# A two-block network on one core: retention values turned to token rows by a transpose, each head's mean taken off while the banks are read

## The reference

```python
proj = u @ w_in
rq, rk, rv, rg, a_cq, a_ckv, a_kr, a_gret, a_gmla = jnp.split(proj, SPLIT_IDX, axis=-1)
rv = rv.reshape(B, L, RET_HEADS, RET_DV)
y_ret = _head_group_norm(_bidir_retention(rq, rk, rv, decay_f, decay_b), gn_w)
y_ret = (jax.nn.silu(rg) * y_ret) @ w_ret_out

def _head_group_norm(y, w):
    mu = jnp.mean(yf, axis=-1, keepdims=True)
    var = jnp.mean(jnp.square(yf - mu), axis=-1, keepdims=True)
    yn = ((yf - mu) * lax.rsqrt(var + GN_EPS)).reshape(B, L, H * dv)
```

## Time and profile before

| | us |
|---|---|
| median of 3 runs | 1061.37 |
| lowest and highest of them | 1061.02, 1061.76 |
| the profiled execution, its own time | 1061.51 |
| its span, first to last instruction | 1059.7 |

### The profile page before, as it was taken

One profiled execution on the slowest core, in us unless ns is written; L12 is line 12 of the kernel. 1 busy time (PEld: TensorE's weight loads), 2 busy tenths in 40 slices (PEclk: granted clock), 3 DMA queues, 4 the chain that ended last, 5 costly groups with the idle time before them and its releaser, 6 DMA issues.

```text
span 1059.7 us, 19331 instructions
## 1 busy us (share of the span) xinstructions
PE 1041.0 (98%) x7716; PEld 963.7 (91%) x7716; DVE 745.9 (70%) x810; ACT 548.0 (52%) x589; POOL 2.2 (0%) x5
## 2 busy tenths in 40 slices
PE   8999999999999999999999999999999999999998
PEld 7998997899999999989889999999898997888887
DVE  6855747768766666678767766666788987766673
ACT  6422536545644444465796444444576574444442
POOL 0000000000000000000000000000000000000000
PEclk8999999999999999999999999999999999999999
DMA  9894242345556666666416455465353444646531
GB/s 304 234 205 147 80 140 80 120 140 166 170 173 180 191 195 196 186 201 224 134 41 238 159 195 201 158 207 190 120 160 120 163 156 158 236 160 204 192 119 40
DMA packets 162589, 177.11 MB, mean 167 GB/s; under 512 B 4800, under 2 KB 148288, under 8 KB 162536
## 3 DMA queue, kind: packets, MB, share of 16 engines
q1 hardware_dynamic: 160704, 174.06, 51.5%
q10 hardware_dynamic: 1832, 2.30, 1.2%
HBM read 174.78 MB, written 1.57 MB: 166 GB/s over the span
## 4 chain that ended last, share of the span: by engine, by line
PE 82%; DVE 11%; ACT 4%; issue 1%; DMA 1%; SPq 0%; DVEq 0%; ACTq 0%
PE proj L466 38%; PE aux L910 13%; PE proj L476 11%; PE aux L932 8%; PE proj L475 5%; DVE wlo L1727 4%; DVE f L1727 2%; DVE f L1730 2%; ACT whi L1244 1%; DVE u L1730 1%; PE aux L663 1%; DVE x_all L1727 1%; DMA f<-in_x_dram 1%; PE aux L778 1%; PE aux L763 1%
## 5 line engine op out<-in xcount | busy, mean ns | idle before, releaser
L1727 DVE TENSOR_TENSOR wlo<-raw,whi 128x2048 fp32r<-128x2048 f32 (+2 forms) x179 | 374.6, 2093 | 100.8 <-ACT whi L1244 88.5
L466 PE MATMUL proj<-u,whi 128*128 128x256 f32 (+1 forms) x1888 | 345.4, 285 | 1.5 <-DVE u L1730 0.7
L1244 ACT ACTIVATE whi<-raw 128x2048 fp32r<-128x2048 f32 (+2 forms) x172 | 309.6, 1800 | 69.4 <-PE proj L466 41.9
L466 PEld LDWEIGHTS proj<-u,whi 128*128 128x128 f32 x1888 | 291.5, 189 | 8.3 <-issue 6.5
L466 PE MATMUL proj<-u,wlo 128*128 128x256 f32 (+1 forms) x944 | 266.2, 282 | 0.0
L476 PE MATMUL proj<-u,whi 128*128 128x512 f32 x512 | 179.7, 393 | 0.0
L466 PEld LDWEIGHTS proj<-u,wlo 128*128 128x128 f32 x944 | 178.5, 189 | 0.0
L910 PE MATMUL aux<-v,whi 128*128 128x256 f32 x864 | 154.3, 280 | 0.8 <-DVE v L1727 0.8
L475 PE MATMUL proj<-u,wlo 128*128 128x256 f32 x512 | 143.7, 281 | 0.9 <-DVE u L1730 0.9
L910 PEld LDWEIGHTS aux<-v,whi 128*128 128x128 f32 x864 | 133.0, 188 | 1.9 <-issue 1.2
L910 PE MATMUL aux<-v,wlo 128*128 128x256 f32 x432 | 120.9, 280 | 0.0
(11 more groups left out here) (307 smaller groups left out, 1065.2 us busy)
## 6 DMA issues: line engine op xcount, KB each, us to landing
raw<-in_mlp_w_dram SPq DMA_DIRECT2D x64, 1024.0 KB, 5.5
raw<-in_w_in_dram SPq DMA_DIRECT2D x21, 1024.0 KB, 7.5
raw<-in_od_w_in_dram SPq DMA_DIRECT2D x12, 1024.0 KB, 5.3
raw<-in_w_ffn_gate_dram SPq DMA_DIRECT2D x22, 512.0 KB, 3.9
raw<-in_w_ffn_up_dram SPq DMA_DIRECT2D x22, 512.0 KB, 5.2
raw<-in_w_ffn_down_dram SPq DMA_DIRECT2D x21, 512.0 KB, 5.4
raw<-in_ev_w_in_dram SPq DMA_DIRECT2D x10, 1024.0 KB, 5.5
raw<-in_w_ret_out_dram SPq DMA_DIRECT2D x4, 1024.0 KB, 5.3
```

The source lines that it names most:

```text
L466: ins = mm(o, w_of(a, k), x_of(b, k), start=first and k == 0 and j == 0, stop=last and k == kt - 1 and j == 2, skip_group_check=skip)
L1244: A.post(act(slot(whi, n, 0, wd), slot(raw, n, 0, wd), ACT.Copy), "hi_ready")
L1727: return ve.tensor_tensor(o, a, b, op)
```

## The change

```diff
@@ -620,8 +620,8 @@
                     if b == hh == 0:
                         read_out("rv3")
                     for q in range(4):
-                        ins = mm(aux[:, 2 * b + hh, q * P:(q + 1) * P], rv_feat[:, 4 * hh + q, META + b * P:META + (b + 1) * P],
-                                 C("centre"), start=True, stop=True)
+                        ins = nc.tensor.transpose(aux[:, 2 * b + hh, q * P:(q + 1) * P],
+                                                  rv_feat[:, 4 * hh + q, META + b * P:META + (b + 1) * P], C("ident"))
                     ins.then_inc(sems["rv_turned"], 1)
             pe.wait_ge(sems["rv_tok_ready"], 1)
             for h in range(HEADS):
@@ -1862,7 +1862,11 @@
             pump(index["c0"])
             for j in range(4):
                 eng.wait_ge(sems["rv_turned"], j + 1)
-                B.post(ve.tensor_copy(rv_tok[:, j // 2, 512 * (j % 2):512 * (j % 2 + 1)], aux[:, j, :]), "rv_tok_ready")
+                by_value = aux[:, j, :].rearrange("p (h n) -> p h n", h=4)
+                B.run(ve.reduce_sum(stat[:, 0:4], by_value, AX_X))
+                B.run(ts(stat[:, 0:4], stat[:, 0:4], 1.0 / P, ALU.mult))
+                B.post(tt(rv_tok[:, j // 2, 512 * (j % 2):512 * (j % 2 + 1)].rearrange("p (h n) -> p h n", h=4), by_value,
+                          stat[:, 0:4][:, :, None].to_broadcast([P, 4, P]), ALU.subtract), "rv_tok_ready")
             eng.wait_ge(sems["rv_turned"], 5)
             B.post(ve.tensor_copy(rv_meta, aux[:, 0, 0:S].rearrange("p (a t) -> p a t", a=2)), "rv_tok_ready")
             b = arrive("c1")
```

## The result

| | before | changed |
|---|---|---|
| median us, first comparison (8 runs each) | 1061.51 | 1064.82 |
| lowest and highest us | 1060.95, 1062.21 | 1063.75, 1066.08 |
| median us, second comparison (26 and 8 runs) | 1061.78 | 1064.98 |
| span of the profiled execution | 1059.7 | 1063.0 |
| mean granted clock of that execution | 0.997 | 0.995 |

The medians lie 3.3 us apart in the first comparison and 3.2 us in the second. The ratio is 1.003 (95% interval 1.0021 to 1.0039) and 1.0025 (1.0015 to 1.0036); it is not the quotient of the medians, and 1.0025 stands for 2.7 us. So the change costs about 3 us. 1063.5 was forecast, with 1064.3 as the upper end.

The account below looks back on a forecast made before the run. TensorE, busy 98%, was taken as the bound, with VectorE's first bank deciding the changed stretch. Wait +0.93 and half clock +1.25 gave +2.2 us on 1061.37, about 1063.5 us; 8-in-10 range 1061.9 to 1064.3.

Parts of the forecast that it names:

- The path: Between c0 and the meta rows, VectorE's first bank decides; the 1.8 us saved on TensorE becomes idle time.
- VectorE's group: First bank's sum 0.69 us, scaling 0.17, subtraction 0.69 (0.75 for the range): 1.62 us against 0.69, +0.93 us.
- The later banks: VectorE's other three banks: +2.8 us hidden in slack; c1's takeover a microsecond late, but nobody waits for it at once.
- The fall of the clock: TensorE's clock falls to half around the wait before the meta rows; with the wait, chance 0.60, 1062.9 to 1064.4 us.
- the transposes join the idle time: Transposes do not count as TensorE being busy: 1.8 us of them plus 3.0 us idling make a fall expected.
- with 2.8 us again: +1.25 us: Cost of half clock after TensorE resumes at the meta rows, lasting 2.8 us as at the program's start: +1.25 us.
- The rate of 0.45 us: TensorE's loss for each microsecond at half clock, from three passes taking 0.64 us against 0.35 at full clock.
- a bound for the cost: Upper bound of 3.1 us for the fall, if the whole 6.8 us of the start were spent on matmuls.
- Given back: Rival: at a later meeting of engines TensorE waits for work not late, so the loss vanishes, 1061.4 us; chance 0.07.

Follow-up runs that it names:

- e2: Changed kernel with TensorE's centring products put back and VectorE's sums, scaling and subtraction kept; median 1062.95 us, beside 1061.99 before.
- e1: Changed kernel with 12 extra unused float32 products on TensorE between the transposes and the wait for the first bank; median 1063.05 us, beside 1061.99 before.
- e11: Changed kernel with 28 further unused transposes of a constant tile in TensorE's wait; median 1062.78 us, beside 1062.12 before.
- e13: Changed kernel with 28 further unused transposes of value blocks in TensorE's wait; median 1063.14 us, beside 1061.98 before.
- e8: Changed kernel with centring products put back and three extra VectorE copies ahead of the first sum; run twice, 1065.48 and 1065.72 us, beside 1061.78 and 1061.98 before.
- e12: Changed kernel with 18 further unused transposes of value blocks and three extra VectorE copies ahead of the first sum; median 1065.56 us, beside 1061.98 before.
- e5: Changed kernel with TensorE's meta rows moved behind c1 and VectorE's meta copy behind the takeover of c1; median 1062.43 us, beside 1061.99 before.
- e3: Changed kernel with VectorE's plain copies put back and the transposes kept; median 1063.50 us, beside 1061.99 before.

## Why the prediction was wrong

- **The path:** right. The first bank on VectorE decides, and the 1.8 us saved on TensorE became idle time.
- **VectorE's group:** right. The sum took 691 ns, the scaling 0.17 us, the subtraction with its spread operand 0.69 us and not 0.75. The wait added 0.93 us here and in e2.
- **The later banks:** right, hidden. VectorE waited 0.62 us for `c1` where I had it a microsecond late, since the half clock delayed TensorE too. At full clock (e1, e2) it went from the split to `c1` without waiting, as I had it, and still delayed nobody.
- **The fall of the clock:** right that it comes, wrong in its chance and in its reason. I gave it 0.60; both profiles have it, and the mean clocks of all 16 executions speak for it. I let the transposes join the idle time; e11 and e13 show that transposes hold the clock. That a fall came was therefore in part luck: with 3 us of idling behind twice the work (e8, e12) it comes in some executions and not in others.
- **The step that failed** is the term "with 2.8 us again: +1.25 us". I took the length of the half-clock stretch from the one case at the start, from TensorE's resuming to the clock's return. Measured, the half clock on matmuls lasted 3.4 us in one profile and 6.1 in the other, and 1.57 and 2.74 us were lost. The rate of 0.45 us was right. The same start showed a low stretch of 6.8 us as a whole; I used it as a bound for the cost and then gave it no chance. With the measured lengths the sum is 2.5 to 3.7 us in place of 2.2, and the measured 3.2 and 3.3 lie between.
- **Given back:** did not happen; what lies behind the stretch takes the same 969.3 to 969.7 us.

## What to carry to other kernels

Time taken off TensorE while another engine ends the wait is not neutral: it turns into idle time, and a few microseconds of that can cost the clock for longer than the wait itself, here 1.6 to 2.7 us on top of 0.9. When a faster step meets an unchanged wait, first move what waits behind work that is ready, then check the next meeting of the two engines; the same change made the kernel 3.2 us slower in one order of work and 2.0 us faster in another. If a stretch at half clock is in the forecast, take the whole length seen in the trace into the range.

## What the runs showed of the hardware that was not expected

- Sixteen float32 transposes of 128x128 are 16 instructions 0.11 us apart; the same products against a constant are 32.
- The kernel before spreads over 3 us, and the start has a large part in it. Its 33 executions in one group run from 1060.53 to 1063.73; the six slowest are exactly those with a mean clock of 0.995, the fastest has 0.998. The program ahead of line 623 is the same in all profiles, yet it starts between 72.75 and 75.05 us: at 72.75 where the clock was low for 3.4 us at the start (e5), at 73.5 to 74.3 where for 6.8 us, at 75.05 where for 10.2 us (e3; the first inputs landed late too, line 572 starts at 7.33 us and not at 5.99). Which of these an execution without a profile had can only be guessed from its mean clock.
